# Up projections with tokens stationary and 512 moving weight columns; the split weights of a half are handed over in two pieces

## What is computed

```python
D_MODEL, SEQ, D_FF = 1024, 256, 2816
def swiglu(h, w_up, w_down):
    gate, up = jnp.split(h @ w_up, 2, axis=-1)      # w_up: 1024 x 5632
    return (jax.nn.silu(gate) * up) @ w_down        # w_down: 2816 x 1024
x = x + 0.5 * swiglu(rmsnorm(x, g), w_up, w_down)
```

## Time and profile before

| | us |
|---|---|
| median of 3 runs | 2115.14 (2113.79 to 2115.72) |
| profiled execution: span from first to last instruction | 2033.4 |
| median less the span | 81.7 |
| TensorE busy | 1783.2 (88%) |
| VectorE busy | 1357.8 (67%) |
| GpSimd busy | 916.9 (45%) |
| ScalarE busy | 773.9 (38%) |

### The profile page before, as it was taken

One profiled execution on the slowest core, in us unless ns is written; L12 is line 12 of the kernel. 1 busy time (PEld: TensorE's weight loads), 2 busy tenths in 40 slices (PEclk: granted clock), 3 DMA queues, 4 the chain that ended last, 5 costly groups with the idle time before them and its releaser, 6 DMA issues.

```text
span 2033.4 us, 29632 instructions
## 1 busy us (share of the span) xinstructions
PE 1783.2 (88%) x11398; PEld 1470.3 (72%) x11398; DVE 1357.8 (67%) x2186; ACT 773.9 (38%) x1248; POOL 916.9 (45%) x859
## 2 busy tenths in 40 slices
PE   7999999999999999989999889779788777777676
PEld 6999999999999999989999788666333332332222
DVE  5778855787377747667764576479899975544444
ACT  5444344544354435565443356333333231211111
POOL 5545620164016350112635012056777777777771
PEclk9999999999999999999999799889989899999999
DMA  7785644566467664346766344378999999999996
GB/s 232 224 293 187 197 156 166 176 208 214 166 191 231 210 203 142 124 140 191 225 215 196 95 148 148 104 279 323 409 409 409 409 409 409 410 410 409 410 409 254
DMA packets 248263, 515.46 MB, mean 253 GB/s; under 512 B 16049, under 2 KB 157666, under 8 KB 248162
## 3 DMA queue, kind: packets, MB, share of 16 engines
q0 software_dynamic: 83024, 301.01, 38.7%
q1 hardware_dynamic: 164466, 211.92, 31.3%
q10 hardware_dynamic: 672, 1.18, 0.2%
HBM read 508.81 MB, written 5.26 MB: 253 GB/s over the span
## 4 chain that ended last, share of the span: by engine, by line
PE 51%; DVE 16%; POOL 11%; DMA 10%; issue 7%; ACT 5%; SPq 0%; ACTq 0%; DVEq 0%; POOLq 0%
PE PX L651 8%; PE PX L653 8%; PE PX L652 8%; PE P L651 6%; PE P L653 6%; PE P L652 6%; DMA late_u<-in_peer_u,M 4%; DVE WL L1665 4%; POOL early_u L620 3%; POOL early_v L620 3%; POOL late_u L620 3%; PE P L1158 3%; ACT WH L1217 3%; DMA early_v<-in_peer_v,M 2%; POOL late_v L620 2%
## 5 line engine op out<-in xcount | busy, mean ns | idle before, releaser
L651 PE MATMUL PX<-hTh,WH 128*128 128x256 f32 x1600 | 462.8, 289 | 27.1 <-DVE WL L1665 15.5
L1665 DVE TENSOR_TENSOR WL<-WR,WH 128x2048 fp32r<-128x2048 f32 x134 | 320.7, 2393 | 220.2 <-ACT WH L1217 220.0
L652 PE MATMUL PX<-hTl,WH 128*128 128x256 f32 x1600 | 457.1, 286 | 0.0
L653 PE MATMUL PX<-hTh,WL 128*128 128x256 f32 x1600 | 456.9, 286 | 0.0
L1217 ACT ACTIVATE WH<-WR 128x2048 fp32r<-128x2048 f32 x134 | 255.8, 1910 | 349.9 <-PE P L653 224.6
L651 PEld LDWEIGHTS PX<-hTh,WH 128*128 128x128 f32 x1600 | 311.7, 195 | 33.3 <-issue 16.5
L1158 PE MATMUL P<-early_v,M 128*128 128x512 f32 x544 | 260.3, 635 | 81.2 <-DMA early_v<-in_peer_v,M 69.9
L652 PEld LDWEIGHTS PX<-hTl,WH 128*128 128x128 f32 x1600 | 311.9, 195 | 0.8 <-issue 0.7
L653 PEld LDWEIGHTS PX<-hTh,WL 128*128 128x128 f32 x1600 | 311.6, 195 | 0.0
L1158 PE MATMUL P<-late_v,M 128*128 128x512 f32 x480 | 228.9, 633 | 77.8 <-DMA late_v<-in_peer_v,M 60.9
L651 PE MATMUL P<-actH,WH 128*128 128x256 f32 x992 | 284.9, 287 | 2.8 <-DVE WL L1665 1.8
(11 more groups left out here) (333 smaller groups left out, 3146.6 us busy)
## 6 DMA issues: line engine op xcount, KB each, us to landing
WR<-in_ffn_w_up SPq DMA_DIRECT2D x88, 1024.0 KB, 7.6
WR<-in_ffn_w_down SPq DMA_DIRECT2D x44, 1024.0 KB, 6.4
adaW<-in_w_ada POOLq DMA_DIRECT2D x48, 512.0 KB, 4.8
WR<-in_diff_w_in SPq DMA_DIRECT2D x14, 1024.0 KB, 7.0
WR<-in_w_in SPq DMA_DIRECT2D x13, 1024.0 KB, 7.0
WR<-in_mem_w_kv SPq DMA_DIRECT2D x8, 1024.0 KB, 6.6
WR<-in_peer_wq SPq DMA_DIRECT2D x8, 1024.0 KB, 8.3
WR<-in_pool_w_in SPq DMA_DIRECT2D x6, 1024.0 KB, 6.4
```

The lines of the kernel that those rows point to most:

```text
L651: mm(o, wh, xh, start=first, stop=False, skip_group_check=skip)
L652: mm(o, wh, xl, start=False, stop=False, skip_group_check=skip)
L653: return mm(o, wl, xh, start=False, stop=last, skip_group_check=skip)
L1665: tt(split_view(WL, U % 2, kind), raw(c % 2, kind, h), split_view(WH, U % 2, kind).bitcast(F32), ALU.subtract)\
```

## The change

The four up phases are turned round. The tokens are now stationary (128 of them, 128 features) and the weights move: a half holds four of the eight feature tiles for all 512 columns of its chunk (256 gate, 256 up), and 128 tokens take 12 matmuls of 512 moving columns from it, both token tiles 24. A chunk's results lie tokens on partitions, in two banks of one token tile each. The inverse deviation is then one number per partition (`rtok`); ScalarE's silu reads PSUM with it as a scale, VectorE's product reads PSUM with it as a scalar, and the pass into `GUP` is gone. The down phase still needs features on partitions, so TensorE transposes each chunk's product, four 128x128 transposes (`act_transposes`), inside the next chunk's second half, for the last chunk behind the first half of the down phase; ScalarE and VectorE split it from the bank, 512 columns at a time. The matmul with the sums of squares becomes two of one column (`token_sums`). The split of a half is made in two pieces of 1,024 columns on each engine, with counts of their own (`hi_part`, `lo_part`); TensorE starts a half on its first piece.

```diff
@@ names
-    GUP = view(0, 2, 2, T)
+    rtok = small[:, 60:62]
...
+    parts_before = {}
+    for u, (c, h) in enumerate(half_of):
+        if chunks[c][0] == "pair":
+            parts_before[u] = len(parts_before)
...
@@ TensorE
+        def token_sums(name):
...
+            for t in range(2):
+                last = mm(P[3][:, t:t + 1], NT[:, 0, t * 128:t * 128 + 128], ones[:, 0:1], start=True, stop=True)
+            last.then_inc(S["ss_ready"], 1)
+
+        def up_product(u, e, h, kk, t):
+            k, o = 4 * h + kk, P[4 + (e + t) % 4][:]
+            w = slice(kk * 512, kk * 512 + 512)
+            xh, xl = hTh[:, k, t * 128:t * 128 + 128], hTl[:, k, t * 128:t * 128 + 128]
+            mm(o, xh, WH[:, u, w], start=(k == 0), stop=False)
+            mm(o, xh, WL[:, u, w], start=False, stop=False)
+            return mm(o, xl, WH[:, u, w], start=False, stop=(k == KT - 1))
+
+        def act_transposes(E, bank):
+            pe.wait_ge(S["bank_free"], E + 2)
+            for j in range(2):
+                for t in range(2):
+                    last = nc.tensor.transpose(bank[:, j * T + t * 128:j * T + t * 128 + 128], PRD[:, t, j * 128:j * 128 + 128], ident[:])
+            last.then_inc(S["act_tr"], 1)
+
+        def up_chunk(U, u, E, e, n, before):
+            pe.wait_ge(S["lo_part"], n + 1)
+            for t in range(2):
+                pe.wait_ge(S["bank_free"], E + t - 3)
+                for kk in range(4):
+                    if t == 0 and kk == 2:
+                        pe.wait_ge(S["lo_ready"], U + 1)
+                    last = up_product(u, e, 0, kk, t)
+            last.then_inc(S["half_used"], 1)
+            pe.wait_ge(S["lo_part"], n + 2)
+            for kk in range(4):
+                if kk == 2:
+                    pe.wait_ge(S["lo_ready"], U + 2)
+                last = up_product(1 - u, e, 1, kk, 0)
+            last.then_inc(S["tile_done"], 1)
+            before()
+            for kk in range(4):
+                last = up_product(1 - u, e, 1, kk, 1)
+            last.then_inc(S["half_used"], 1)
...
+            first_chunk(U, E, NORMS[f"up{i}{f}"][2])
+            token_sums(f"up{i}{f}")
...
             for v in range(p["n"]):
-                pe.wait_ge(S["act_lo"], FT * (2 * i + f) + 2 * v + 2)
+                pe.wait_ge(S["act_lo"], c0 + (CHUNKS if v >= 2 else CHUNKS - 1))
...
                 rows_half(p["U"] + v, 2 * v, v == 0, v == FT // 2 - 1)
+                if v == 0:
+                    act_transposes(E + FT - 2, P[4 + (E + FT - 4) % 4])
@@ ScalarE
-            nc.scalar.activation(split_view(WH, U % 2, "pair"), raw(c % 2, "pair", h), copy).then_inc(S["hi_ready"], 1)
+            nc.scalar.activation(WH[:, U % 2, 0:1024], WR[:, c % 2, h * 2048:h * 2048 + 1024], copy).then_inc(S["hi_part"], 1)
+            nc.scalar.activation(WH[:, U % 2, 1024:2048], WR[:, c % 2, h * 2048 + 1024:h * 2048 + 2048], copy).then_inc(S["hi_ready"], 1)
...
-            nc.scalar.activation(SIL[:, j % 2], GUP[:, j % 2, 0], ACT.Silu).then_inc(S["sil_ready"], 1)
+            nc.scalar.activation(SIL[:, t], P[4 + (e + t) % 4][:, 0:T], ACT.Silu, scale=rtok[:, t:t + 1]).then_inc(S["sil_ready"], 1)
...
-            nc.scalar.activation(tile, PRD[:, j % 2], copy).then_inc(S["act_hi"], 1)
+            act.wait_ge(S["act_tr"], c + 1)
+            nc.scalar.activation(tiles, bank[:], copy).then_inc(S["act_hi"], 1)
...
+                    split_loop(U + 2 * c + 2, r)
+                    act.wait_ge(S["tile_done"], r * 2 + (c0 + c + 1))
+                    gate_silu(r * 4 + (E + 2 * c), E + 2 * c, 0)
+                    hi_act(r * 2 + (c0 + c - 1), P[2 + (c - 1) % 2],
...
+                    split_loop(U + 2 * c + 3, r)
+                    gate_silu(r * 4 + (E + 2 * c), E + 2 * c, 1)
@@ VectorE
-                tt(GUP[:, j % 2], P[4 + (E + j) % 4][:].rearrange("p (a b) -> p a b", a=2),
-                   rstd[:].unsqueeze(1).broadcast_to([128, 2, T]), ALU.mult).then_inc(S["bank_free"], 1)
...
-                tt(PRD[:, j % 2], SIL[:, j % 2], GUP[:, j % 2, 1], ALU.mult).then_inc(S["prod_ready"], 1)
...
-                tt(lo, PRD[:, j % 2], hitile.bitcast(F32), ALU.subtract).then_inc(S["act_lo"], 1)
...
+                stt(PRD[:, t], P[4 + (e + t) % 4][:, T:2 * T], rtok[:, t:t + 1], SIL[:, t], ALU.mult, ALU.mult).then_inc(S["bank_free"], 1)
...
+                tt(lo, bank[:], hi.bitcast(F32), ALU.subtract).then_inc(S["act_lo"], 1)
...
+                    split_loop(U + 2 * c + 2, r)
...
+                    lo_act(r * 2 + (c0 + c - 1), P[2 + (c - 1) % 2], one[0], one[1])
+                    product(r * 4 + 2 * (c0 + c), E + 2 * c, 0, r * 2 + (c0 + c))
+                    split_loop(U + 2 * c + 3, r)
+                    product(r * 4 + 2 * (c0 + c), E + 2 * c, 1, r * 2 + (c0 + c))
```

More of the change, by code:

```diff
@@ L751, in statistics @@
                 pe.wait_ge(S["sqs_ready"], m + 1)
[L752 to L757, removed]
+                mm(P[6][:, 0:T], ones[:], NT[:, 0], start=True, stop=True).then_inc(S["ss_ready"], 1)
@@ L759, in ffn, with transposes @@
         def ffn(i, f, after_first=None, before_down=None):
-            first_halves(f"up{i}{f}")
+            p = phases[f"up{i}{f}"]
+            U, E, c0 = p["U"], p["E"], CHUNKS * (2 * i + f)
+            first_chunk(U, E, NORMS[f"up{i}{f}"][2])
+            token_sums(f"up{i}{f}")
             if after_first:
                 after_first()
[L763 to L767, removed]
+            def transposes(c, r=0):
+                if c >= 2:
+                    pe.wait_ge(S["act_lo"], r * 2 + (c0 + c - 1))
+                elif i == f == c == 0:
+                    pe.wait_ge(S["mem_in"], 4)
+                act_transposes(r * 4 + (E + 2 * c), P[2 + c % 2])
@@ new lines, in lo_act, with lo, step @@
+            def lo_act(c, bank, lo, hi):
+                dve.wait_ge(S["act_hi"], c + 1)
+                tt(lo, bank[:], hi.bitcast(F32), ALU.subtract).then_inc(S["act_lo"], 1)
+            def lo(c):
+                lo_act(c0 + c, P[2 + c % 2] if c < CHUNKS - 1 else P[4 + (E + FT - 4) % 4],
+                       *(b[:, 2 * c:2 * c + 2].rearrange("p a t -> p (a t)") for b in (actL, actH)))
+            def step(c):
+                split(U + 2 * c + 2)
+                lo(c - 1)
+                product(2 * (c0 + c), E + 2 * c, 0, c0 + c)
+                split(U + 2 * c + 3)
+                product(2 * (c0 + c), E + 2 * c, 1, c0 + c)
@@ new lines, in ffn @@
+            split(U + 2)
+            split(U + 3)
+            token_rstd(f"up{i}{f}")
+            for t in range(2):
+                dve.wait_ge(S["sil_ready"], 2 * c0 + t + 1)
+                if c0 and t == 0:
+                    dve.wait_ge(S["act_tr"], c0)
+                stt(PRD[:, t], P[4 + (E + t) % 4][:, T:2 * T], rtok[:, t:t + 1], SIL[:, t], ALU.mult, ALU.mult).then_inc(S["bank_free"], 1)
+            with dve.Fori(0, 4) as r:
+                for c in (1, 2):
+                    split_loop(U + 2 * c + 2, r)
+                    one = [b[:, bass.ds(r * 4 + (2 * c - 2), 2), :].rearrange("p a t -> p (a t)") for b in (actL, actH)]
+                    lo_act(r * 2 + (c0 + c - 1), P[2 + (c - 1) % 2], one[0], one[1])
+                    product(r * 4 + 2 * (c0 + c), E + 2 * c, 0, r * 2 + (c0 + c))
+                    split_loop(U + 2 * c + 3, r)
+                    product(r * 4 + 2 * (c0 + c), E + 2 * c, 1, r * 2 + (c0 + c))
@@ L1820, in ffn @@
+            for c in (9, 10):
+                step(c)
+            lo(CHUNKS - 1)
             p = phases[f"down{i}{f}"]
```

160 lines of the change are left out of this document (79 added, 81 removed).

## The result

The changed kernel takes 2101.25 us (median of 4 runs, 2096.75 to 2104.09) against 2114.47 us beside it (2113.17 to 2115.72): a ratio of 0.9923, interval 0.9905 to 0.994. That is 13 us or 0.8% faster; 43 us had been forecast, and the time lies above the range. In a later comparison on another chip the ratio was 0.9937 (0.9914 to 0.9961), 15 us.

A forecast was written before the change was run, and what follows sets the result against it. TensorE's own matmul pace was taken to bound the up phases; gains of 38.35 (up01, up10, up11) and 6.8 (up00), less 1.8 for down-phase transposes, gave 43.4 us: span 1990.0, plus 81.7 around it, 2071.7 us; range 2066 to 2095.

The forecast's parts named there:

- The pace of a wide matmul: Up phases: a 512-column float32r matmul starts every 0.216 us, bounds 0.213 to 0.240, against 0.120 for 256 columns.
- The argument from half clock: A 256-column float32r matmul at half clock starts every 0.21 us, exactly its stream, so float32r streams no slower by nature.
- Rival B: Up matmuls: the 0.013 us is a fixed cost per float32r matmul, 0.2265 each, 22.2 us less gain, 2093.9 us; 12%.
- C: Up matmuls: float32r stream limited at full clock, 512 columns take 0.240 us, kernel slower at 2122.4 us; 6%.
- D: Up chunks beside GpSimd's work: TensorE's transposes wait for VectorE's late product, 0.5 us a chunk, 2087 us; 7%.
- E: Chunk transposes cost 0.213 us each, as at half clock, or draw the clock down: 18.3 us, 2090 us; 3%.
- F: Stages are bound elsewhere, by raw weights landing later or by `ada`; the time hardly moves, 2110 to 2116 us; 2%.
- Transposes: Four new per chunk on TensorE, 0.11 us each: 4.4 us per up phase, 0.44 per down phase, 19.2 in all.
- Waits removed: Up phases: with splits handed over in two pieces, the waits of 4 to 5 us a phase go.
- The wait for the root: In up00 TensorE idles some 3.5 us before the memory's transposes; root at 34 us, second chunk starting at about 35.8.
- Item (4): Raw weights land in 7.6 us, at most 10.5; about 11 us until the next read, 16 until TensorE misses them.
- The last stage: What follows the up and down phases is untouched and moves as a whole, its length unchanged.

The follow-up runs named there:

- the probe: A separate kernel of back-to-back matmuls by width and type, computing nothing of the reference; float32r starts 0.227 us apart at 512 columns, 0.120 at 256.
- the narrow kernel: The changed kernel with each 512-column up matmul made as two of 256 columns: 2123.9 us, 1.0054 of the kernel before.

## Why the prediction was wrong

**The pace of a wide matmul, the largest term, was mis-sized.** The step took 0.216 us from the nearest row, a plain float32 record that streams as long; measured 0.2265, in the changed kernel and by itself. 2,112 matmuls x 0.0105 are 22.2 us of the 25.9 that are missing at the last projection (43.4 forecast, 17.5 measured between the two profiles; against the repeat of the kernel before 12.5 are measured and 30.9 missing). The clue stood in the same rows. A 4-column float32r matmul starts every 0.11 us, a 256-column one every 0.120: neither load nor stream makes up the 0.120, and the rest was let go. The argument from half clock, where no extra is seen, was no argument: a cost of 0.013 beside a stream can disappear at 1.2 GHz, and does. Rival B was this case exactly, mechanism and price, and it got 12%.

**Rivals.** B's 2093.9 kept every other term at its best. Of the 7 us above it the profiles show 3.7: 2.8 in up00, 2.3 in the three later up phases, less 1.4 in the stages between. The rest lies within the 5 us by which the first profile of before reached the last projection later than its repeat. C is excluded by the probe: the extra does not grow with width. D did not come: TensorE is never idle before the transposes of a chunk. E is excluded by the transposes made twice. F named what came in small: raw weights land late in up00.

**Transposes: right.** 0.11 each, no cost in clock, 4.4 us a phase. The 275 ns in E are no rival price: one record lasts 0.27 us here too (the earlier trace rows and the 0.60 above), while the starts are 0.11 apart, and it is the starts that cost.

**Waits removed: right.** No wait in up01, up10 and up11. The pieces alone gave 12.1 us in these phases, the forecast having seen 14.3 of waits there with the heads. VectorE is busy 14 to 23 us less in each of them, near the 20 forecast.

**What is left in the later up phases.** 528 x 0.2265 + 4.4 + 0.3 are 124.3 us, and 125.0 are measured. Of the 0.7 some 0.4 is that the mean of the wide starts is 0.2273: about one in nine, most of them soon behind the transposes, comes after 0.229 to 0.236. The rest is small change: 0.36 for the one-column matmuls, 0.45 for the transposes of a chunk, and rounding.

**up00: one step right, one wrong.** The wait for the root came as reckoned. That the second chunk started at 36.1 for 35.8 is partly luck: the root was there at 33.1 and not 34, and the transposes behind it then ran at half clock, 3.4 us for 1.9 in the earlier trace rows, which had not been seen. Item (4), that raw weights have 5 us and more in hand, took the landing time from the up loads inside the loops and overlooked GpSimd's 4 MB store, which stands in the trace of before:

```profile
125.50 1.14 POOL L536 DMA_DIRECT2D rel_rows<-M  x1 [0.30 <-POOL adaS L527]
```

There the first down weights beside it took 10.1 and 12.2 us to land and nothing waited for them. In the changed kernel they took 16 us; TensorE lost 2.0 us, and the down phase then began at less than full clock, 0.67 from 152.2 to 154 us and 0.72 from 154 to 158.

**The last stage.** Unchanged on the faster chip, as forecast. On the slower ones it differs by up to 8 us between executions, and the stages ahead of it by some 5, so that 17.5 or 12.5 in pairs of profiles and 13 in the medians do not contradict each other.

**What was gained, then.** The two pieces alone account for 8 us by the medians, rather more than half of the whole; the turned product alone for nothing that can be measured; both for 13 to 15. In the three later up phases alone each part gives 12 us and both give 18.6. Why the turned product alone loses its 12 us again elsewhere is not shown.

## What to carry to other kernels

Where a stream and a load are equally long and neither explains the pace, the rest is a cost of its own until a run shows otherwise; price a wider instruction with it and without it, and let the smaller gain be the forecast. A handover cut in two lets the next step start on the first piece and costs only a few instructions: try it alone before turning a product round, which here had to pay 4.4 us of transposes out of 6.5 from its width. And when a phase gets shorter, ask what large transfer lies beside its last loads, since it need not move with them.

## What the runs showed of the hardware

A float32r matmul costs 0.013 us beside its stream at full clock, a float32 record or a bfloat16 matmul 0.002 to 0.003; at half clock the float32r extra is not seen (0.427 for 512 columns, 0.213 for 256). From 192 columns down a float32r matmul with its load starts every 0.111 us; a bfloat16 one of 128 columns starts every 0.056.

In the probe the clock fell in a stretch without a gap. There 32 float32r matmuls of 64 columns, 0.112 apart, stood ahead of the 32 of 4 columns, and TensorE was busy throughout (columns: window, length, busy of PE, PEld, ACT and POOL, granted clock, DMA share, GB/s):

```profile
57.00:64.00 7.00, 7.00 (x66) 7.00 (x64) 0.00 (x0) 0.00 (x0) 1.00 0.00 0
64.30:67.90 3.60, 3.60 (x34) 3.60 (x33) 0.00 (x0) 0.00 (x0) 0.97 0.02 5
68.00:74.70 6.70, 6.70 (x34) 6.70 (x33) 0.00 (x0) 0.00 (x0) 0.50 0.00 0
```

At 0.50 it is 1.2 GHz, and it came back during the wide matmuls that followed. The 16 transposes in up00 took 1.94 us at full clock after a wait of 0.66 or 0.44 us. After one of 3.42 they took 3.41 us in the changed kernel and 2.62 in its repeat, with the clock at 0.50 for most or a part of them, but in the narrow kernel the clock stayed at 1.00 after the same wait:

```profile
34.81 1.94 PE L928 MATMUL P<-ident,M 128*128 128x128 f32 x16 [3.42 <-ACT small L1341]
```

So the length of that wait alone does not say whether the clock falls.

One store of 4 MB from GpSimd delays the load of raw weights that lies beside it, wherever the store was put: to 12.2 us until landing in the kernel before and to 16 to 18 in the changed ones, from a median of 7.6. In four parts of 1 MB, in one profile, it cost TensorE nothing.
